# Expert weights laid out in advance: one transfer of gate and up and one of down per expert, in a ring of three places

## The reference

```python
x2: (512, 1024);  w_gate, w_up: (2, 32, 1024, 512);  w_down: (2, 32, 512, 1024)
scores = sigmoid(x2 @ router_w)
expert, gates = the best group of 4 experts, and in it the best 2, per token
for each expert e, on the rows that chose it:
    h = silu(xblk @ w_gate[e]) * (xblk @ w_up[e])
    y = h @ w_down[e]
out[token] += gate * y
x = layer_norm(ALPHA * x + out)
```

## Time and profile before

| | |
|---|---|
| median of 3 runs | 1558.73 us (1558.11 to 1559.13) |
| span of the profiled execution, first to last instruction | 1556.0 us |
| mean granted TensorE clock in it | 0.950 |
| PE busy | 1416.5 us (91%) |
| DVE, ACT, POOL busy | 501.0, 282.4, 53.3 us |
| bytes moved by DMA | 463.73 MB, mean 298 GB/s |
| transfers of gate, up, down of 2048 KB | 60, 60, 62, with 18.7, 23.2, 24.2 us from issue to landing (median) |

### The profile page before, as it was taken

One profiled execution on the slowest core, in us unless ns is written; L12 is line 12 of the kernel. 1 busy time (PEld: TensorE's weight loads), 2 busy tenths in 40 slices (PEclk: granted clock), 3 DMA queues, 4 the chain that ended last, 5 costly groups with the idle time before them and its releaser, 6 DMA issues. The chain is left out here.

```text
span 1556.0 us, 16022 instructions
## 1 busy us (share of the span) xinstructions
PE 1416.5 (91%) x6550; PEld 789.5 (51%) x6550; DVE 501.0 (32%) x1028; ACT 282.4 (18%) x483; POOL 53.3 (3%) x68
## 2 busy tenths in 40 slices
PE   6999885999999999998799997593999999999996
PEld 5878672444443444334587876473444344434431
DVE  2355653121221221221444218745121221221222
ACT  3222320010110110111443123421001110110111
POOL 1000010000000000000000000010000000000000
PEclk9999986999999999999899988795999999999998
DMA  8530547999999999999131120428899999999995
GB/s 247 189 82 0 203 175 272 413 422 420 420 421 421 420 421 421 422 421 346 55 108 55 55 108 1 190 78 348 367 422 420 420 422 420 421 421 420 422 421 210
DMA packets 96533, 463.73 MB, mean 298 GB/s; under 512 B 10952, under 2 KB 31432, under 8 KB 47304
## 3 DMA queue, kind: packets, MB, share of 16 engines
q1 hardware_dynamic: 91848, 454.26, 72.3%
q0 software_dynamic: 4608, 8.40, 1.4%
HBM read 458.44 MB, written 12.58 MB: 303 GB/s over the span
## 5 line engine op out<-in xcount | busy, mean ns | idle before, releaser
L990 PE MATMUL bank<-ring,xT 128*64 128x512 f32 x2048 | 455.8, 598 | 9.0 <-DMA ring<-in_w_up 7.3
L990 PEld LDWEIGHTS bank<-ring,xT 128*64 128x64 f32 x2048 | 143.3, 137 | 275.3 <-issue 258.4
L1030 PE MATMUL bank<-ring,hidT 128*64 128x512 f32 x1024 | 235.9, 602 | 1.7 <-issue 1.1
L1213 DVE COPY xT<-bank 128x512 f32<-128x512 f32 x64 | 44.3, 692 | 499.0 <-PE bank L972 499.0
L972 PEld LDWEIGHTS bank<-x_sb 128*128 128x128 f32 x512 | 124.1, 327 | 69.0 <-issue 47.0
L972 PE MATMUL bank<-x_sb 128*128 128x128 f32 x512 | 136.0, 412 | 21.7 <-DMA x_sb<-x_rows,tok_of_slot 21.7
L1030 PEld LDWEIGHTS bank<-ring,hidT 128*64 128x64 f32 x1024 | 68.2, 137 | 159.0 <-issue 156.7
L1143 ACT COPY y<-bank 128x512 f32<-128x512 f32 x64 | 37.6, 587 | 401.8 <-PE bank L1030 401.8
L1137 ACT ACTIVATE hid<-bank 128x256 f32<-128x256 f32 x64 | 24.5, 383 | 440.1 <-PE bank L990 440.1
L1223 DVE COPY hidT<-bank 128x256 f32<-128x256 f32 x64 | 27.1, 423 | 184.9 <-PE bank L1004 184.9
L1047 PE MATMUL bank<-y,x_sb 64*128 64x512 f32 x256 | 72.3, 641 | 1.4 <-ACT y L1143 1.4
(11 more groups left out here) (270 smaller groups left out, 1441.9 us busy)
## 6 DMA issues: line engine op xcount, KB each, us to landing
ring<-in_w_down SPq DMA_DIRECT2D x62, 2048.0 KB, 24.2
ring<-in_w_gate SPq DMA_DIRECT2D x60, 2048.0 KB, 18.7
ring<-in_w_up SPq DMA_DIRECT2D x60, 2048.0 KB, 23.2
ring<-in_mlstm_w_in SPq DMA_DIRECT2D x6, 2048.0 KB, 7.7
ring<-in_conv_w_in SPq DMA_DIRECT2D x18, 512.0 KB, 6.5
ring<-in_w_out SPq DMA_DIRECT2D x2, 4096.0 KB, 14.4
ring<-in_w_gate SPq DMA_DIRECT2D x8, 1024.0 KB, 28.7
ring<-in_w_up SPq DMA_DIRECT2D x8, 1024.0 KB, 27.9
```

What stands on the lines that cost most here:

```text
L990: last = nc.tensor.matmul(GU_BANK[e % 2][64 * f:64 * f + 64, :], xgT[e // 2 % 2][:, 4 * h + c, 64 * (e % 2):64 * (e % 2) + 64], gu[:, :, h ...
L1030: last = nc.tensor.matmul(Y_BANK[e % 2][64 * n:64 * n + 64, :], hidT[e % 2][:, c, 64 * f:64 * f + 64], dn[:, f, c, 512 * n:512 * n + 512], ...
L1213: V.tensor_copy(xgT[q % 2][:, 4 * h:4 * h + 4, :], o[:, :].rearrange("p (c r) -> p c r", c=4)).then_inc(xcopied, 1)
```

## The change

The three arrays `w_gate`, `w_up`, `w_down` are replaced as inputs by one, `w_pack`, of shape (2, 32, 128, 12288). It is made on the host from the same numbers before the launch: for each layer and expert, partition p's whole place of the ring lies there in one piece of 48 KB. Gate and up of an expert become one transfer of 4 MB with one run of 32 KB per partition, down one of 2 MB with a run of 16 KB. The pieces of the last two experts' gate and up are 2 MB with runs of 16 KB (before: 1 MB of gate and 1 MB of up, runs of 8 KB), those of the last down remain 1 MB with runs of 8 KB. SP waits for the same things before it issues. PE waits for 16 counts where it waited for 32.

Within a place, rows are dealt out otherwise: partition p now holds row 128c + p for step c, so `turn_rows` and `turn_hidden` read 128 neighbouring floats instead of every fourth or second one. The moving operand of `gate_up` is 512 neighbouring floats, 256 of gate and 256 of up, where it was two pieces of 256. The places of the ring, the semaphores, the number of matmuls and their order stay.

```diff
         def expert_views(r):
             part = ring[:, r * W_EXP:(r + 1) * W_EXP]
-            gu = part[:, 0:2 * W_MAT].rearrange("p (m h c f) -> p m h c f", m=2, h=2, c=4)
+            gu = part[:, 0:2 * W_MAT].rearrange("p (h c f x) -> p h c f x", h=2, c=4, f=2)
...
         def load_gate_up(eng, l, e, r, done):
-            part = ring[:, r * W_EXP:r * W_EXP + 2 * W_MAT].rearrange("p (m h x) -> p m h x", m=2, h=2)
-            for m, w in ((0, w_gate), (1, w_up)):
-                src = w[l, bass.ds(e, 1)].rearrange("o (h p c) f -> p (o h) (c f)", h=2, p=P)
-                eng.dma_start(part[:, m], src).then_inc(done, 16)
+            src = w_pack[l, bass.ds(e, 1)].rearrange("o p x -> p (o x)")
+            eng.dma_start(ring[:, r * W_EXP:r * W_EXP + 2 * W_MAT], src[:, 0:2 * W_MAT]).then_inc(done, 16)

         def load_down(eng, l, e, r, done):
-            part = ring[:, r * W_EXP + 2 * W_MAT:(r + 1) * W_EXP].rearrange("p (f x) -> p f x", f=2)
-            src = w_down[l, bass.ds(e, 1)].rearrange("o (f p c) d -> p (o f) (c d)", f=2, p=P)
-            eng.dma_start(part, src).then_inc(done, 16)
+            src = w_pack[l, bass.ds(e, 1)].rearrange("o p x -> p (o x)")
+            eng.dma_start(ring[:, r * W_EXP + 2 * W_MAT:(r + 1) * W_EXP], src[:, 2 * W_MAT:]).then_inc(done, 16)
...
                             for h in range(2):
-                                for m, w in ((0, w_gate), (1, w_up)):
-                                    sp.dma_start(gu[:, m, h], w[l, e, 512 * h:512 * h + 512].rearrange("(p c) f -> p c f", p=P)
-                                                 ).then_inc((in_gu[l][r], late_gu[r])[h], 16)
+                                z = slice(h * W_MAT, (h + 1) * W_MAT)
+                                sp.dma_start(ring[:, r * W_EXP:(r + 1) * W_EXP][:, z], w_pack[l, e][:, z]
+                                             ).then_inc((in_gu[l][r], late_gu[r])[h], 16)
...
                         def turn_rows(k):
-                                last = nc.tensor.matmul(o[:, c * P:(c + 1) * P], xg[g % 3][:, 512 * h + c:512 * h + 512:4],
+                                last = nc.tensor.matmul(o[:, c * P:(c + 1) * P], xg[g % 3][:, 512 * h + c * P:512 * h + (c + 1) * P],
...
                         def gate_up(e, halves=(0, 1)):
-                                pe.wait_ge(in_gu[l][r], 32 * (e // 3 + 1))
+                                pe.wait_ge(in_gu[l][r], 16 * (e // 3 + 1))
...
-                                                                gu[:, :, h, c, 256 * f:256 * f + 256],
+                                                                gu[:, h, c, f, :],
...
                         def turn_hidden(e):
-                                last = nc.tensor.transpose(H_BANK[:, c * P:(c + 1) * P], hid[e % 2][:, c::2], ident[:, :])
+                                last = nc.tensor.transpose(H_BANK[:, c * P:(c + 1) * P], hid[e % 2][:, c * P:(c + 1) * P], ident[:, :])
...
 def kernel(**inputs):
+    pack = _np.empty((DEPTH, N_EXPERTS, P, W_EXP), _np.float32)
+    gu = _np.empty((DEPTH, N_EXPERTS, P, 2, 4, 2, 2, 256), _np.float32)
+    for m, name in enumerate(('w_gate', 'w_up')):
+        w = _np.asarray(inputs[name]).reshape(DEPTH, N_EXPERTS, 2, 4, P, 2, 256)
+        gu[:, :, :, :, :, :, m] = w.transpose(0, 1, 4, 2, 3, 5, 6)
+    pack[:, :, :, 0:2 * W_MAT] = gu.reshape(DEPTH, N_EXPERTS, P, 2 * W_MAT)
```

More of the change, by code:

```diff
@@ L62, in build_trunk @@
 def build_trunk(nc, x, mem, conv_w_in, conv_w, mlstm_w_in, mlstm_gate_b, mlstm_norm_g, w_kv_mem, w_out,
-                ln1_g, ln1_b, ln2_g, ln2_b, router_w, router_b, w_gate, w_up, w_down, out, stop=99):
+                ln1_g, ln1_b, ln2_g, ln2_b, router_w, router_b, w_pack, out, stop=99):
     ctx = ExitStack()
@@ L909, in _ @@
                         for r, e in ((0, LAST - 1), (1, LAST)):
-                            gu, dn = expert_views(r)
+                            dn = expert_views(r)[1]
                             sp.wait_ge(gu_done, e - 2)
                             for h in range(2):
-                                for m, w in ((0, w_gate), (1, w_up)):
-                                    sp.dma_start(gu[:, m, h], w[l, e, 512 * h:512 * h + 512].rearrange("(p c) f -> p c f", p=P)
-                                                 ).then_inc((in_gu[l][r], late_gu[r])[h], 16)
+                                z = slice(h * W_MAT, (h + 1) * W_MAT)
+                                sp.dma_start(ring[:, r * W_EXP:(r + 1) * W_EXP][:, z], w_pack[l, e][:, z]
+                                             ).then_inc((in_gu[l][r], late_gu[r])[h], 16)
                             sp.wait_ge(y_done, e - 3)
@@ L919, in _ @@
                         for f in range(2):
-                            sp.dma_start(dn[:, f], w_down[l, e, 256 * f:256 * f + 256].rearrange("(p c) d -> p c d", p=P)
+                            sp.dma_start(dn[:, f], w_pack[l, e][:, 2 * W_MAT:].rearrange("p (f c d) -> p f c d", f=2, c=2)[:, f]
                                          ).then_inc((in_dn[l][1], last_dn)[f], 16)
@@ L979, in gate_up @@
                             if halves == (1,):
-                                pe.wait_ge(late_gu[r], 32)
+                                pe.wait_ge(late_gu[r], 16)
                             else:
-                                pe.wait_ge(in_gu[l][r], 32 * (e // 3 + 1))
+                                pe.wait_ge(in_gu[l][r], 16 * (e // 3 + 1))
                                 pe.wait_ge(xcopied, 2 * (e // 2) + 2)
@@ L1374, in step @@
                     for c in range(4):
-                        last = nc.tensor.transpose(bank[1][:, c * P:(c + 1) * P], xg[:, c::4], ident[:, :])
+                        last = nc.tensor.transpose(bank[1][:, c * P:(c + 1) * P], xg[:, c * P:(c + 1) * P], ident[:, :])
                     last.then_inc(xturned, 1)
                     pe.wait_ge(xcopied, n + 1)
-                    pe.wait_ge(in_gu1, 32 * (n + 1))
+                    pe.wait_ge(in_gu1, 16 * (n + 1))
                     gu, dn = expert_views(1)
@@ L1388, in step @@
                     for c in range(2):
-                        last = nc.tensor.transpose(bank[3][:, c * P:(c + 1) * P], hid[:, c::2], ident[:, :])
+                        last = nc.tensor.transpose(bank[3][:, c * P:(c + 1) * P], hid[:, c * P:(c + 1) * P], ident[:, :])
                     last.then_inc(hturned, 1)
@@ L2049 @@
 _INS = ['x', 'mem', 'conv_w_in', 'conv_w', 'mlstm_w_in', 'mlstm_gate_b', 'mlstm_norm_g', 'w_kv_mem', 'w_out',
-        'ln1_g', 'ln1_b', 'ln2_g', 'ln2_b', 'router_w', 'router_b', 'w_gate', 'w_up', 'w_down']
+        'ln1_g', 'ln1_b', 'ln2_g', 'ln2_b', 'router_w', 'router_b']
 def kernel(**inputs):
@@ L2059 @@
     arrays, args = {}, []
-    for name in _INS:
-        a = _np.ascontiguousarray(inputs[name])
+    laid = {name: inputs[name] for name in _INS}
+    pack = _np.empty((DEPTH, N_EXPERTS, P, W_EXP), _np.float32)
[4 more added lines that the diff above has]
+    pack[:, :, :, 0:2 * W_MAT] = gu.reshape(DEPTH, N_EXPERTS, P, 2 * W_MAT)
+    w = _np.asarray(inputs['w_down']).reshape(DEPTH, N_EXPERTS, 2, 2, P, D_MODEL)
+    pack[:, :, :, 2 * W_MAT:] = w.transpose(0, 1, 4, 2, 3, 5).reshape(DEPTH, N_EXPERTS, P, W_MAT)
+    laid['w_pack'] = pack
+    for name, a in laid.items():
+        a = _np.ascontiguousarray(a)
         arrays[f"in_{name}"] = a
```

## The result

The changed kernel takes 1541.32 us (median of 4 runs, 1539.06 to 1543.45), the kernel before, timed beside it, 1558.42 us (4 runs, 1556.60 to 1559.13). The ratio is 0.9893, with a 95% interval of 0.9878 to 0.9908: 17.1 us faster, where 10.8 were forecast. The time lies in the range (1538 to 1557), 6.6 us under the predicted one. The profiled execution has a span of 1537.3 us, before 1556.0.

A forecast was written before the change was run, and what follows sets the result against it. DMA's weight stream and PE were both taken as nearly full, the stream setting each layer's end. Stream 9.0, loads before it 0.6, first turns 0.6 and hole 0.6 made 10.8 us, giving 1547.9 us, range 1538 to 1557.

The forecast's parts named there:

- Stream: Expert weight loads of each layer: 904 fewer packets per engine save 4.5 us per layer, 9.0 us in all.
- I take 5 ns: Fixed time per DMA packet in the weight loads, taken as a mean of 3.3, 3.7 and 8.3 ns.
- First turns: The 16 counted matmuls before each layer's first `gate_up` get shorter with neighbouring floats: 0.3 us per layer, bounds 0 and 1.9.
- Hole: Layer 0's weight stream, a window at 389 GB/s where SP waits for PE: closing it gives 0.6 us, bounds 0 and 0.8.
- Loads before the stream: Early expert loads of each layer, with the first gather at their end: 64 fewer packets save 0.3 us per layer.
- PE at 13.3 us per expert and always waiting, over 70 us: PE outpaces the weight stream's 14.86 us per expert, waits on every expert, and is busy for about 90%.
- PEclk at 1.00 in the waits: PE's granted clock during the stream: waits of some 1.6 us per expert would not lower it.
- Rival (a): `turn_rows` isn't slow because of its step, so PE stays slow and only its present waits are gained: 1550.9 us, chance 0.06.
- (b): Weight stream: long packets are no faster, 421 GB/s is what the path gives: 1557.5 us, chance 0.12.
- (d): Weight stream: long packets move at a lower rate, deciding from 1245 ns per 32 KB packet: 1580.5 us, chance 0.10.
- Rival (c): First gather of each layer takes turns with 32 KB weight packets and lands later: 14.7 us more, 1562.6 us, chance 0.04.

The follow-up runs named there:

- The curve above: Changed kernel with all packets 4 KB (1577.93 us), 8 KB, 16 KB (1545.71 us) or its own 32 and 16 KB: 409, 421, 427, 429 GB/s.
- the kernel built to be that rival: Changed kernel's long packets, but rows dealt out and PE's steps of four and two floats as in the kernel before: 1546.35 us, ratio 0.9937.
- late down: Third expert's down weights issued after the first gather has landed: 1529.55 us on the changed kernel, 1548.63 us on the kernel before.
- blocks: Changed kernel with each expert's weights in DRAM as six blocks of 128 pieces of 8 KB, so packets have 8 KB: 1557.1 us, ratio 0.9992.
- padding: Changed kernel with 256 bytes of padding after every 8 KB in DRAM, so packets have 8 KB at nearly the changed kernel's addresses: 1556.61 us, ratio 0.9993.
- all packets: Changed kernel with 256 bytes of padding after every 16 KB, so gate, up and down all have 16 KB packets: 1545.71 us, ratio 0.9925.

## Why the prediction was right, and what was sized wrong

**Stream, 2 x 4.5 us forecast, 2 x 7.9 measured: the term that was off.** 904 packets fewer per engine and layer was right (17228 of 8 KB and more remain; the forecast 16600 had counted the experts that come in halves as whole), and so was that they count in full, since the end goes with the stream. The step that failed is "I take 5 ns": the fixed time is 9 ns. It stood in my bounds as 8.3 ns, from the window of 4 KB runs at 410 GB/s; I averaged that with 3.3 from the 2 KB window and 3.7 from the 416 GB/s one. The 3 to 8 us windows were too short to give a rate to 1%, while 12 GB/s between 4 and 8 KB was the whole question. 904 x 9 = 8.1 us is what the profile has, 7.9 in layer 1. The Trainium skill, "DMA: Bandwidth & Descriptors", section "Why small descriptors are slow (HBM only)", has about 3 cycles of fixed overhead per packet; by that page's fabric clock of 850 MHz this is an estimate of 3.5 ns. The curve above contradicts it with 9 ns. Joining 8 KB runs is worth 16 us here.

**First turns, 2 x 0.3 us forecast.** 4.10 us became 3.48 and 3.68: 0.6 and 0.4. **Hole, 0.6 us.** It is gone; with it layer 0's stream gained 9.1 us against 7.9 in layer 1, 1.2 more. **Loads before the stream, 2 x 0.3 us.** Not seen: the first gather's issue lies between 242.1 and 246.3 us in the twelve profiles, whatever the packets, so 0.3 us can't be read.

**The sum.** 9.1 + 7.9 for the streams with the hole and 0.6 + 0.4 for the first turns, less 0.2 + 1.0 for slower first gathers, are 16.8 us of the 17.1. The gathers were at nothing in the prediction. The time fell into the range because the range's low end was built with the 8.3 ns; the 5 ns that gave the forecast were an average of rows that couldn't settle it.

**PE at 13.3 us per expert and always waiting, over 70 us.** The pace is right (13.2), and `turn_rows` takes 1.09 us as expected. Its loads take 199 ns, not 140, those of `turn_hidden` 141:

```profile
L969 PEld LDWEIGHTS bank<-x_sb 128*128 128x128 f32 x512 | 64.9, 199 | 70.1 <-issue 47.1 <-DMA x_sb<-x_rows,tok_of_slot 23.1
L1001 PEld LDWEIGHTS bank<-ident,hid 128*128 128x128 f32 x128 | 14.4, 141 | 25.2 <-issue 24.3 <-DVE hid L1214 0.8
```

The waits are 41.7 us, not 70, and PE is busy for 95% of the stream, not 90: I had applied the pace of the stream to all experts, but PE starts with three in the ring and uses up that lead at 1.5 us per expert, so it doesn't wait before 1269 in layer 1, at expert 15 (453 in layer 0, the same expert). Nothing in the time hangs on it.

**PEclk at 1.00 in the waits.** Wrong: it is 0.83 in the window behind a wait of 1.88 us and 0.68 behind one of 3.12, and the `gate_up` there takes 8.78 and 9.93 us instead of 7.09. The earlier trace rows had a wait of 1.25 us only. But the length of the wait doesn't decide it alone:

```profile
529.67 7.09 PE L987 MATMUL bank<-ring,xT 128*64 128x512 f32 x32 [1.88 <-DMA ring<-in_w_pack]
...
1450.16 7.09 PE L987 MATMUL bank<-ring,xT 128*64 128x512 f32 x32 [2.04 <-DMA ring<-in_w_pack]
```

In the second profile of this kernel one behind 3.20 us took 7.09 us too. In both profiles no `gate_up` behind a wait of 1.75 us or less was slow. It costs nothing while the weights are late anyway; PE's busy time for `gate_up` grew from 455.8 to 463.2 us, of 41.7 us of slack.

**Rival (a), PE stays slow, 1550.9.** PE didn't stay slow, but the kernel built to be that rival took 1546.35, so its price was wrong. "Only as far as PE waits now, 7.3 us and a few tenths for down" left out the 1.45 us for `in_mem` that the prediction itself names, and 1.7 us of slower clock behind that wait. Of the 11.9 us measured 10.7 are found; the rest is less than the measurement's uncertainty of 3 us.

**Rivals (b) and (d), long packets no faster or slower.** Refuted by the windows, and by the curve over four lengths. (d) began at 1245 ns per packet of 32 KB; the median one takes 1215.

**Rival (c), the gather stuck behind long packets, +14.7 us.** The mechanism exists, its size on the path is small. Time from the issue of the first gather to PE's first turn, in us, beside the third expert's down:

| beside it | layer 0 | layer 1 |
|---|---|---|
| nothing (late down, changed kernel, two profiles) | 3.8, 3.8 | 3.8, 5.2 |
| nothing (late down, kernel before) | 3.7 | 4.4 |
| 4 KB | 7.2 | 7.0 |
| 8 KB (before, blocks, padding) | 8.4, 8.5, 8.9 | 8.3, 8.3, 8.2 |
| 16 KB (all packets) | 9.7 | 9.0 |
| 16 KB, behind 32 KB (changed kernel, two profiles; rows as before) | 8.6, 8.9, 9.1 | 9.3, 9.7, 10.3 |

In the run with 5.2 us a last 32 KB packet of the loads ahead still started 3.0 us after the gather's issue. The middle of a layer, where the whole stream runs beside the gathers, shows the effect of the length more clearly: the median of all 16 gathers of a profile lands 7.4 us after its issue beside 4 KB packets, 8.3 and 8.4 beside 8 KB, 10.7 beside 16 KB and 13.3 beside 32 and 16 KB. Nobody waits for those.

The records of the packets show the turns: in the changed kernel, per us from 1065 to 1068, there start 8, 19, 40 and 70 packets of the gathers beside 22, 24, 10 and 4 of 16 KB; the gather gets its pace when the down runs out. They also show what the turns don't explain. Beside the down the gather's first packet starts 4.2 to 4.9 us after its issue, whatever the weights' packets are, and without it 1.8 to 1.9: about 2.5 of the 4 to 6 us are this later start, and what holds it isn't shown. And a gather has 128 slots but moves only 64 rows on average (2048 packets of 4 KB for 32 gathers and scatters), 4 per engine, not the 8 that the prediction took.

The prediction argued that the gather ends with the stream of the loads, whatever the packets' length, and 8 to 9 us was right but for 0.3 to 0.7. What it took as given, the 8 us, was the real loss: 4 to 6 us per layer, in the kernel before too. The Trainium skill, "DMA: Bandwidth & Descriptors", section "Queues, rings and completion order", has an engine take turns between its queues packet by packet; the landing times by packet length and the counts agree.

## What to carry to other kernels

Where one queue of weights sets the end, count its packets: here each costs 9 ns beyond its bytes, and 8 KB runs were still worth joining to 16 and 32 KB, for 1.4 and 1.9% more rate. Such a gain arrives only as far as the consumer is ahead, so give it room in the same edit, and sum every wait that ends with the stream, not only the largest group, when you price it. And look for a small transfer that the path waits for while a large one, not needed yet, shares the engines: moving that one behind it gave 12 us for one line, where the change itself gave 16 to 17.

## What the runs showed that I had not expected

- A gather of 4 KB rows into 128 partitions reaches PE 3.7 to 5.2 us after its issue with no transfer issued beside it, and after 7 to 10 us beside 2 MB of weights.
- In the middle of a layer POOL waits for its scatters to land before it may gather again, up to 15.7 us, before up to 9.3: the long packets beside them do cost them time. Nobody else waits for them here, and a kernel with less room would see it.
- Behind waits of 1.8 to 3.2 us PE's next `gate_up`, 7.09 us at full clock, took up to 9.93 in some cases and 7.09 in others; behind shorter waits it was slow in none of ten profiles.
- SP spends 0.33 us on an issue of 4 MB now, where it spent 0.4 on one of 2 MB. A transfer of 6 MB instead of 4 and 2 cost 150 us, though it has fewer packets; the chain puts that down to the coarser release of the ring's places.
